# One core, two decoder layers: U's clear and load moved up behind the attention, and four shorter moves in the queues

## The reference, cut to what matters

```python
h = rmsnorm(x, p['norm_g'])
u_a, z_a, u_b, z_b, q, z_x, g_a, g_b, g_x = jnp.split(h @ p['w_in'], IN_SPLITS, axis=-1)
# A: diagonal state space, 32 groups x 16 channels, complex state of 64 per group
bu = einsum('blgh,gph->blgp', u, b_bar)
xs = scan(lam_bar, bu) + a_cum * s0
y_a = gelu(real(einsum('blgp,ghp->blgh', xs, c)) + d * u)
y_a = y_a * sigmoid(y_a @ w_glu + b_glu)
o_a = (y_a * silu(z_a)) @ w_br_ssm
# B: gated causal depthwise convolution of 31 taps, LayerNorm
o_b = (silu(layernorm(conv(u_b0 * sigmoid(u_b1)))) * silu(z_b)) @ w_br_conv
# X: 4 heads of attention into 256 memory rows (samples: their own key and value caches)
o_x = (softmax(q k^T) v * silu(z_x)) @ w_br_xatt
m = sigmoid(g_a) * o_a + sigmoid(g_b) * o_b + sigmoid(g_x) * o_x
x = x + m @ w_out
```

## Time and profile before

| | us |
|---|---|
| median of 3 runs | 1162.32 |
| lowest and highest of them | 1159.71, 1163.30 |
| time of the profiled execution | 1161.13 |
| its span in the profile | 1159.3 |

### The profile page before, as it was taken

One profiled execution on the slowest core, in us unless ns is written; L12 is line 12 of the kernel. 1 busy time (PEld: TensorE's weight loads), 2 busy tenths in 40 slices (PEclk: granted clock), 3 DMA queues, 4 the chain that ended last, 5 costly groups with the idle time before them and its releaser, 6 DMA issues.

```text
span 1159.3 us, 20485 instructions
## 1 busy us (share of the span) xinstructions
PE 1084.3 (94%) x8274; PEld 1015.6 (88%) x8274; DVE 834.0 (72%) x1209; ACT 415.8 (36%) x709; POOL 427.9 (37%) x329
## 2 busy tenths in 40 slices
PE   5999899989989899999989999998998999899995
PEld 3679889979979889999956999897997989899994
DVE  3899989868996684444677998987899668644412
ACT  5423443325443252222433354332535334222222
POOL 0245443524332223444403644353332331344440
PEclk9999999989999999999999999999998999899998
DMA  9345427594317813445532651669531573344422
GB/s 259 100 100 189 145 74 213 191 167 121 99 42 148 231 62 115 130 129 155 152 98 82 173 181 50 196 205 168 133 110 56 124 182 119 103 123 136 135 83 74
DMA packets 225269, 155.01 MB, mean 134 GB/s; under 512 B 48651, under 2 KB 201675, under 8 KB 223111
## 3 DMA queue, kind: packets, MB, share of 16 engines
q1 hardware_dynamic: 219590, 142.04, 44.4%
q10 hardware_dynamic: 5584, 11.67, 2.8%
HBM read 130.38 MB, written 24.24 MB: 133 GB/s over the span
## 4 chain that ended last, share of the span: by engine, by line
PE 51%; DVE 31%; SPq 6%; DMA 6%; issue 4%; ACT 2%; POOL 0%; DVEq 0%; ACTq 0%
PE acc L729 29%; PE mp L1071 12%; DVE cacc L1457 10%; DVE s L1451 4%; DVE X L1451 3%; DMA w_st<-in_w_in 3%; PE mp L768 2%; SPq L464 2%; PE mp L659 2%; DVE tiny L1451 2%; PE acc L1052 1%; SPq L505 1%; PE mp L874 1%; DVE wt L1451 1%; DMA y_scratch<-U 1%
## 5 line engine op out<-in xcount | busy, mean ns | idle before, releaser
L610 POOL TENSOR_TENSOR w_lo<-w_st,w_hi 128x512 fp32r<-128x512 f32 x288 | 403.3, 1406 | 654.4 <-ACT w_hi L1148 654.0
L1148 ACT CAST w_hi<-w_st 128x512 fp32r<-128x512 f32 x288 | 177.6, 622 | 574.1 <-PE acc L729 352.8
L729 PE MATMUL acc<-h_hi,w_hi 128*128 128x260 f32 x1600 | 332.0, 289 | 6.8 <-ACT z L1293 5.9
L729 PE MATMUL acc<-h_hi,w_lo 128*128 128x260 f32 x1600 | 325.2, 285 | 0.0
L729 PE MATMUL acc<-h_lo,w_hi 128*128 128x260 f32 x1600 | 325.1, 285 | 0.0
L729 PEld LDWEIGHTS acc<-h_hi,w_hi 128*128 128x128 f32 x1600 | 250.8, 191 | 15.8 <-issue 7.7
L729 PEld LDWEIGHTS acc<-h_lo,w_hi 128*128 128x128 f32 x1600 | 249.9, 191 | 0.0
L729 PEld LDWEIGHTS acc<-h_hi,w_lo 128*128 128x128 f32 x1600 | 249.9, 191 | 0.0
L1457 DVE SCALAR_TENSOR_TENSOR cacc<-vx,cw,cacc 128x512 f32<-128x512 f32 x232 | 222.7, 1021 | 10.3 <-POOL w_lo L610 7.0
L1071 PE MATMUL mp<-br_hi,w_hi 128*128 128x260 f32 x384 | 79.1, 288 | 6.2 <-DVEq L1933 3.9
L1071 PE MATMUL mp<-br_lo,w_hi 128*128 128x260 f32 x384 | 78.7, 287 | 0.0
(11 more groups left out here) (300 smaller groups left out, 1408.2 us busy)
## 6 DMA issues: line engine op xcount, KB each, us to landing
w_st<-in_w_in SPq DMA_DIRECT2D x208, 256.0 KB, 3.2
g_scratch<-xT ACTq DMA_DIRECT2D x32, 260.0 KB, 3.2
xT<-g_scratch SPq DMA_DIRECT2D x8, 1040.0 KB, 6.6
kb<-in_cache_mem_k SPq DMA_DIRECT2D x16, 512.0 KB, 4.2
kb<-in_cache_mem_v SPq DMA_DIRECT2D x16, 512.0 KB, 5.1
w_st<-in_w_out SPq DMA_DIRECT2D x32, 256.0 KB, 2.8
x_scratch<-xT SPq DMA_DIRECT2D x2, 2080.0 KB, 7.6
xT<-x_scratch SPq DMA_DIRECT2D x4, 1040.0 KB, 5.9
```

The lines of the kernel that those rows point to most:

```text
L610: pool.tensor_tensor(w_lo[:, slot, :], w_st[:, slot, :], w_hi[:, slot, :].bitcast(F32), ALU.subtract).then_inc(w_staged_free, 1)
L729: last = pe.matmul(acc_ps[pair][:, a, 0:HC], w[:, slot, kk * P:(kk + 1) * P], x[:, k, a, :], start=(k == 0 and p == 0), stop=(k == KT - 1 ...
L1148: act.copy(w_hi[:, c % SLOTS, :], w_st[:, c % SLOTS, :]).then_inc(w_hi_done, 1)
```

## The change

`t1` and `t2` move from U's space to that of the keys, the probabilities and the later `Mt`. POOL clears U behind e0's lows, waiting for `pv_done` only, and waits for `V_done` ahead of the clear of `Mt`. SP loads U in pieces between the halves of e2, x0 and x1, issues the sample's values 0 to 3 one unit later, stores the lags apart from `toeplitz` (the first ahead of e4, the second ahead of a1, with `toeplitz(1)` behind a1's first half). TensorE turns the memory before the parameters, and the square sums stand behind two key products.

```diff
-        t1 = rr("t1", 10256, [P, QH * (T + 1) * H])
-        t2 = rr("t2", 11408, [P, QH * (T + 1) * H])
+        t1 = rr("t1", 6912, [P, QH * (T + 1) * H])
+        t2 = rr("t2", 8064, [P, QH * (T + 1) * H])
...
                 wait(sp, l, "u_ev", 4)
                 sp.dma_start(u_dram...).then_inc(sm["u_out"], 16)
-                pair("e1")
-                half("e2", 0)
-                for b in range(4, NB - 2):
+                def prompt_rows(first, end):
+                    for t in range(first, end):
+                        sp.dma_start(Ug[t * H:(t + 1) * H, :, NB:NB + C], ug[...]).then_inc(sm["U_in"], 16)
+                def sample_rows(a):
+                    sp.dma_start(Ug[0:H, :, 4 * a:4 * a + 4], ug[:, :, a, 4 * C:HC]).then_inc(sm["U_in"], 16)
+                    sp.dma_start(Ug[7 * H:P, :, YC + 4 * a:YC + 4 * a + 4], ug[:, :, a, 4 * C:HC]).then_inc(sm["U_in"], 16)
+                def keys(b):
                     wait(sp, l, "kq_done", b - 3)
                     cache_load(cache_mem_k, b)
+                pair("e1")
+                wait(sp, l, "u_out", 16)
+                wait(sp, l, "U_clear", 1)
+                prompt_rows(0, 3)
+                half("e2", 0)
+                prompt_rows(3, 5)
+                keys(4)
                 half("e2", 1)
-                for b in range(NB - 2, NB):
-                    wait(sp, l, "kq_done", b - 3)
-                    cache_load(cache_mem_k, b)
+                keys(5)
+                prompt_rows(5, 7)
                 half("x0", 0)
+                keys(6)
+                keys(7)
+                prompt_rows(7, 8)
+                sample_rows(0)
+                half("x0", 1)
                 for b in range(2):
                     wait(sp, l, "kq_done", b + 5)
                     cache_load(cache_mem_v, b)
-                half("x0", 1)
+                half("x1", 0)
                 for b in range(2, 4):
                     wait(sp, l, "kq_done", b + 5)
                     cache_load(cache_mem_v, b)
-                half("x1", 0)
+                sample_rows(1)
                 half("x1", 1)
                 half("e3", 0)
                 for b in range(4, NB):
                     wait(sp, l, "pvs_done", b - 3)
                     cache_load(cache_mem_v, b)
-                wait(sp, l, "u_out", 16)
-                wait(sp, l, "U_clear", 1)
-                for t in range(T):
-                    sp.dma_start(Ug[...], ug[...]).then_inc(sm["U_in"], 16)
-                for a in range(2):
-                    sp.dma_start(...)
-                    sp.dma_start(...)
-                def toeplitz(half):
+                def lags_out(half):
                     wait(sp, l, "k_ev", half + 1)
                     sp.dma_start(kh.rearrange("(r y) h x -> (y h) r x", r=2), kt[:, :, :]).then_inc(sm["k_out"], 16)
+                def toeplitz(half):
                     wait(sp, l, "k_out", 16 * (half + 1))
...
                 half("e3", 1)
+                lags_out(0)
                 half("e4", 0)
                 toeplitz(0)
                 half("e4", 1)
...
+                lags_out(1)
+                half("a1", 0)
                 toeplitz(1)
...
-                pair("a1")
+                half("a1", 1)
                 half("b1", 0)
...
-                for name in ("u1", "e0", "e1", "e2", "x0"):
+                for name in ("u1", "e0"):
+                    pair(name)
+                wait(pool, l, "pv_done", 1)
+                pool.memset(U[:, :, :, 0:NB], 0.0)
+                pool.memset(U[:, :, :, YC:UC], 0.0).then_inc(sm["U_clear"], 1)
+                for name in ("e1", "e2", "x0"):
                     pair(name)
                 wait(pool, l, "u_out", 16)
                 pool.memset(psT[:, :, :, :], 0.0).then_inc(sm["psT_clear"], 1)
-                wait(pool, l, "pv_done", 1)
+                pair("x1")
                 wait(pool, l, "V_done", 1)
-                pool.memset(U[:, :, :, 0:NB], 0.0)
-                pool.memset(U[:, :, :, YC:UC], 0.0).then_inc(sm["U_clear"], 1)
-                pair("x1")
                 pool.memset(Mt[:, :, :], 0.0).then_inc(sm["m_clear"], 1)
...
             pe.wait_ge(sm["consts"], 3)
-            param_turns(0)
-            wait(pe, 0, "par_ev", 1)
...
             memory_turns(0)
             memory_turns(1)
+            param_turns(0)
+            wait(pe, 0, "par_ev", 1)
...
-                    key_values(0, 1)
+                    key_values(0, 2)
                     square_sums()
-                    key_values(1, 4)
+                    key_values(2, 4)
```

More of the change, by code:

```diff
@@ L435, in _ @@
                 sp.dma_start(u_dram.rearrange("(i p) a c -> p i (a c)", p=P), u[:, :, :, :].rearrange("p i a c -> p i (a c)")).then_inc(sm["u_out"], 16)
-                pair("e1")
-                half("e2", 0)
-                for b in range(4, NB - 2):
+                ug = u_dram.rearrange("(g h) a c -> h g a c", h=H)
+                Ug = U[:, :, :, :].rearrange("p q e c -> p (q e) c")
+                def prompt_rows(first, end):
+                    for t in range(first, end):
+                        sp.dma_start(Ug[t * H:(t + 1) * H, :, NB:NB + C], ug[:, :, t // 4, (t % 4) * C:(t % 4 + 1) * C]).then_inc(sm["U_in"], 16)
+                def sample_rows(a):
+                    sp.dma_start(Ug[0:H, :, 4 * a:4 * a + 4], ug[:, :, a, 4 * C:HC]).then_inc(sm["U_in"], 16)
+                    sp.dma_start(Ug[7 * H:P, :, YC + 4 * a:YC + 4 * a + 4], ug[:, :, a, 4 * C:HC]).then_inc(sm["U_in"], 16)
+                def keys(b):
                     wait(sp, l, "kq_done", b - 3)
                     cache_load(cache_mem_k, b)
+                pair("e1")
[5 more added lines that the diff above has]
+                keys(4)
                 half("e2", 1)
-                for b in range(NB - 2, NB):
-                    wait(sp, l, "kq_done", b - 3)
-                    cache_load(cache_mem_k, b)
+                keys(5)
+                prompt_rows(5, 7)
                 half("x0", 0)
+                keys(6)
[3 more added lines that the diff above has]
+                half("x0", 1)
                 for b in range(2):
@@ L458, in _ @@
                     cache_load(cache_mem_v, b)
-                wait(sp, l, "u_out", 16)
-                wait(sp, l, "U_clear", 1)
-                ug = u_dram.rearrange("(g h) a c -> h g a c", h=H)
-                Ug = U[:, :, :, :].rearrange("p q e c -> p (q e) c")
-                for t in range(T):
-                    sp.dma_start(Ug[t * H:(t + 1) * H, :, NB:NB + C], ug[:, :, t // 4, (t % 4) * C:(t % 4 + 1) * C]).then_inc(sm["U_in"], 16)
-                for a in range(2):
-                    sp.dma_start(Ug[0:H, :, 4 * a:4 * a + 4], ug[:, :, a, 4 * C:HC]).then_inc(sm["U_in"], 16)
-                    sp.dma_start(Ug[7 * H:P, :, YC + 4 * a:YC + 4 * a + 4], ug[:, :, a, 4 * C:HC]).then_inc(sm["U_in"], 16)
-                def toeplitz(half):
+                def lags_out(half):
                     wait(sp, l, "k_ev", half + 1)
                     kh = k_dram[half * (G // 2):(half + 1) * (G // 2)]
-                    kg = kh.rearrange("g h x -> h g x")
                     sp.dma_start(kh.rearrange("(r y) h x -> (y h) r x", r=2), kt[:, :, :]).then_inc(sm["k_out"], 16)
+                def toeplitz(half):
+                    kg = k_dram[half * (G // 2):(half + 1) * (G // 2)].rearrange("g h x -> h g x")
                     wait(sp, l, "k_out", 16 * (half + 1))
@@ L486, in _ @@
                 half("e4", 1)
[L487 to L491, removed]
+                for name in ("e5", "e6", "e7", "b0", "a0"):
+                    pair(name)
+                lags_out(1)
+                half("a1", 0)
                 toeplitz(1)
```

## The result

The changed kernel takes 1148.38 us in the median of four runs (1143.98 to 1152.10), beside 1161.86 of the kernel before: ratio 0.9884, 95% interval 0.9845 to 0.9923. So it is faster by 8 to 14 us, where 22.4 were forecast. Its four runs spread over 8 us, those of the kernel before, in the same measurement, over 3.6; over more runs the kernel before spreads as far (11.7 us over eleven, beside the control), so the spread is not a mark of the change. One execution of the kernel before, of 2720 us, which fell beside the first four experiments, is left out of their ratios.

The account below looks back on a forecast made before the run. TensorE bounds the kernel, so only its stops can be won: U 14.2 + square sums 4.2 + memory turns 1.4 + lag stores 2.6 = 22.4 off 1161.1, plus 1.2 to the median, gives 1140 us; range 1134 to 1152.

Parts of the forecast that it names:

- what would show it right: Signs: no oxs or layer 1 sum wait, U issued 176 to 216, clock 1.0 near 250, memg at 12.1, a1 before Mt.
- U, 14.2 forecast: Both TensorE stops for oxs before the sample output turns go whole, 8.1 and 6.1 us; ends 0 and 14.2.
- I take 0, since each of the rows ahead has its own 5 us to drain: Keys of products 6 and 7, behind x0's weights and five U rows, cost nothing; bounds 0 and 5 us a layer.
- late keys: Rival, 14%: keys of products 6 and 7 pay the upper bound in both layers, 10 us more, 1150.
- takes the whole shift and keeps some 3.5: VectorE, idle 7.34 and 5.53 us ahead of the second input matrices, follows U's gain with some 3.5 us idle left.
- Square sums, 4.2 forecast: Layer 1: second key product fills TensorE's idle 3.35 us, first pair ends at 609.9 for 614.1; ends 0.9 and 5.1.
- Start, 1.4 forecast: Memory turns no longer wait for parameters, memg at 12.1 for 14.21; term 1.4 us, ends 0 and 1.8.
- only the 1.8 between their end and rs can go: Start: third key weights hold the row factors at 34.4 as before; only the gap from 36.0 to 37.88 can shrink.
- Lag stores and a1, 2.6 forecast: Layer ends: a1's first half issued 7 us sooner, its second 1.4, with GELU, y and b1; 1.3 us a layer.
- 0.3 late, and x_done holds that product anyway: Second outputs: Mt rows, now behind a1's 512 KB, come 0.3 us late at no cost, as the product awaits x_done.
- The lower end, -1.8: Worst end of the lag stores term: Mt 0.9 us late in each layer, nothing regained.
- VectorE's pace: Rival, 10%: VectorE keeps its pace, so square sums give 0.9, start 0, layer ends 1.3; 1146 us.

Follow-up runs that it names:

- the control: The changed kernel measured once more, unedited, on another chip beside the kernel before: ratio 0.9922, median 1151.90 us.
- the first four experiments: U edit alone on the kernel before (0.9914); changed kernel with square sums undone (0.9946), lag stores and a1 weights undone (0.9870), start undone (0.9928).
- the U part alone: The kernel before with only the U edit, the other three edits undone: ratio 0.9914 to the kernel before, runs from 1140.6 to 1155.8 us.

## Why the prediction came out as it did

The forecast was 1140, the range held the time (1148.4), and the sign was right. Nearly every step in "what would show it right" is there. The sum was too large by 5 us against the profiled execution, and by 9 to 14 against the medians. Two of the signs for "wrong" came too: VectorE idle ahead of key product 6, and a TensorE stop between 200 and 245, of 0.67 us in the first profile and 1.49 in the control.

**U, 14.2 forecast, 11.3 in the profile (6.3 and 5.0), some 10 by itself.** The stops went whole. Two steps failed. "I take 0, since each of the rows ahead has its own 5 us to drain": VectorE waited 2.4 and 2.7 us for the key of product 6 in the profile and 5.1 in the control's layer 1. The forecast had the issue right (195.6 for "about 196") and the landing wrong, 7.3 to 8.2 us for 4.2; the row of before that it should have gone by was that of U behind value loads, which it kept as a bound. Its rival *late keys* was thus half true: late always, in the way of TensorE only sometimes. And "takes the whole shift and keeps some 3.5": VectorE kept nothing. Its idle 12.9 us of the earlier trace rows went as 6.3 of shift, 2.6 of key waits and the remaining 4 of slower work. Between 236 and 244 GpSimd had stood idle before, since no weights came; once they flow (3.54 of the 8 us busy), its lows run beside VectorE's taps. Operation by operation the 4 us are five lengthenings of 0.9 to 1.05 us, each where a low runs, less one of 1.1 that is gone from the first matrices. That is read from durations, not isolated by an experiment as in the scan.

**Square sums, 4.2 forecast, 3.6 in the profile, 3.4 when undone.** Right, a little under the size.

**Start, 1.4 forecast, 0.2.** The step "only the 1.8 between their end and rs can go" took the gap for idle time. It is VectorE's chain of small operations on the parameters, which ends just ahead of `rs` in both profiles and starts behind the turned tokens. These did not come sooner, because TensorE now idles ahead of the first key product and runs it at the 1.2 GHz level. Keeping it busy repairs the product; what that would give at the start is open, since the one profile of it has late parameters and late key weights.

**Lag stores and a1, 2.6 forecast, a loss of 2 to 6 us measured.** The ends of the layers gain 2.1 in the profile, but not by this edit: with it undone they gain 4.1. The first link was right (the b1 stop falls from 3.1 to 0.66, where the U part alone leaves 2.57) and the balance wrong. The step that failed is the list of what an early load sets off. It had SP and the DMA queue, Mt "0.3 late, and x_done holds that product anyway", and not ScalarE's cast and GpSimd's lows behind it, which made x_done itself 1.8 us later. Nor did any rival have a stop that the change makes, with the clock behind it. The lower end, -1.8, was too narrow for that.

So by the medians a loss of 2 to 6 us in one part stood against some 10 and 3 of gain in the others, 7 to 11 in all. That the range held is in part luck: its upper end, 1152, was drawn for late keys in full and for VectorE's pace, not for a loss in this part, and the control's 1151.90 is only just inside.

## What to carry to other kernels

A load that is moved forward brings its cast and its low with it: list all three, and ask what VectorE does at that time and who waits for it. Where a stop is won on an engine that stands a few us ahead of the next wait, price the next one with the clock behind it (here up to 4 us for 0.75), since that can outweigh the stop. And where one execution is far faster than the median of its kernel, read a second one before believing its sum.

## What was not expected of the hardware

VectorE operations with both inputs in SBUF can take 0.9 to 1.1 us longer when a GpSimd low of about 1.3 us runs beside them, whatever their length: 0.58 to 1.50 us, 1.24 to 2.17, 0.19 to 1.22, and in the changed kernel's matrices of 1152 columns 1.35 to 2.44. The key products, with one input in PSUM, and their sums kept 1.22 us beside the same lows. The Trainium skill (SBUF — State Buffer, "Who interferes with whom") says that a VectorE instruction with two SBUF inputs contends with a GpSimd instruction that reads SBUF, through a pair of ports that works as an exclusive lock. The trace agrees: the low at 346.37 ends at 347.66, and the operation that began at 346.53 ends at 348.03, as if most of its 0.58 us came after the low.

The length of a stop doesn't tell alone whether the clock falls. Ahead of the second outputs 0.77 us were not followed by a lower granted clock (1.00), 1.40 and 1.52 were (0.50 and 0.52); ahead of the sample products 1.49 and 1.60 were not (1.00), 2.14 was (0.84 in layer 1 of the control, from 779 to 787, and 0.57 in layer 0 of the U part alone, where a stop of 1.39 stood just ahead of it).
